# Half-width tiles and half-width statistics at three norms of a two-block transformer kernel on one NeuronCore

## What is computed

```python
def _rmsnorm(x, g):
    xf = x.astype(jnp.float32)
    y = xf * lax.rsqrt(jnp.mean(xf * xf, axis=-1, keepdims=True) + NORM_EPS)
    return (y * g.astype(jnp.float32)).astype(x.dtype)

        x = x + g1 * y
        h = _rmsnorm(x, norm2_g[i]) * (1.0 + sc2) + sh2
        x = x + g2 * _swiglu(h, ffn_w_gate[i], ffn_w_up[i], ffn_w_down[i])
```

## Time and profile before

| | |
|---|---|
| median of three executions | 1727.47 us |
| the profiled execution | 1725.33 us |
| its span, first to last instruction | 1723.5 us |
| mean granted TensorE clock | 0.994 |
| TensorE matmuls busy | 1685.5 us, 98% |
| VectorE busy | 1015.4 us, 59% |
| ScalarE busy | 702.4 us, 41% |
| GpSimd busy | 77.3 us, 4% |
| TensorE's share of the chain that ended last | 89% |

### The profile page before, as it was taken

One profiled execution on the slowest core, in us unless ns is written; L12 is line 12 of the kernel. 1 busy time (PEld: TensorE's weight loads), 2 busy tenths in 40 slices (PEclk: granted clock), 3 DMA queues, 4 the chain that ended last, 5 costly groups with the idle time before them and its releaser, 6 DMA issues.

```text
span 1723.5 us, 23287 instructions
## 1 busy us (share of the span) xinstructions
PE 1685.5 (98%) x7891; PEld 1342.7 (78%) x7891; DVE 1015.4 (59%) x2004; ACT 702.4 (41%) x1329; POOL 77.3 (4%) x62
## 2 busy tenths in 40 slices
PE   9999999999999998889999999999999999999999
PEld 7677777778887776567888888887888888888887
DVE  7788776665466788835655563467444633333334
ACT  5364776663344335753333323234223433332322
POOL 0020000000000073100000000000000000000000
PEclk9999999999999999999999999999999999999999
DMA  6453344444332121002555553353233233332333
GB/s 242 159 160 113 138 156 147 147 147 153 98 98 62 37 86 38 1 25 74 174 194 193 195 198 121 122 183 87 97 99 98 77 99 96 96 101 93 98 98 110
DMA packets 56776, 202.84 MB, mean 118 GB/s; under 512 B 6576, under 2 KB 6704, under 8 KB 56560
## 3 DMA queue, kind: packets, MB, share of 16 engines
q1 hardware_dynamic: 56688, 201.68, 35.7%
HBM read 198.38 MB, written 2.10 MB: 116 GB/s over the span
## 4 chain that ended last, share of the span: by engine, by line
PE 89%; DVE 6%; ACT 2%; issue 2%; DMA 1%; SPq 0%; POOL 0%; DVEq 0%; ACTq 0%; POOLq 0%
PE bank L481 26%; PE bank L483 25%; PE bank L482 25%; PE bank L608 2%; PE bank L663 2%; PE bank L642 1%; PE bank L524 1%; PE bank L525 1%; DVE W_lo L1466 1%; PE bank L539 1%; DVE SB L2075 1%; DVE AW L1480 1%; PE bank L755 1%; PE bank L774 1%; PE bank L527 1%
## 5 line engine op out<-in xcount | busy, mean ns | idle before, releaser
L481 PE MATMUL bank<-H_hi,W_hi 128*128 128x512 f32 x1336 | 534.0, 400 | 3.4 <-DVE W_lo L1466 2.2
L483 PE MATMUL bank<-H_hi,W_lo 128*128 128x512 f32 x1336 | 521.2, 390 | 0.0
L482 PE MATMUL bank<-H_lo,W_hi 128*128 128x512 f32 x1336 | 521.2, 390 | 0.0
L1466 DVE TENSOR_TENSOR W_lo<-RAW,W_hi 128x512 fp32r<-128x512 f32 x538 | 351.4, 692 | 173.7 <-ACT W_hi L951 157.5
L951 ACT ACTIVATE W_hi<-RAW 128x512 fp32r<-128x512 f32 x538 | 317.2, 625 | 264.7 <-PE bank L483 235.3
L481 PEld LDWEIGHTS bank<-H_hi,W_hi 128*128 128x128 f32 x1336 | 251.3, 188 | 74.0 <-issue 20.0
L482 PEld LDWEIGHTS bank<-H_lo,W_hi 128*128 128x128 f32 x1336 | 251.5, 188 | 54.4 <-issue 4.5
L483 PEld LDWEIGHTS bank<-H_hi,W_lo 128*128 128x128 f32 x1336 | 251.2, 188 | 53.4
L481 PE MATMUL bank<-A_hi,W_hi 128*128 128x512 f32 x352 | 136.9, 389 | 0.0
L483 PE MATMUL bank<-A_hi,W_lo 128*128 128x512 f32 x352 | 136.9, 389 | 0.0
L482 PE MATMUL bank<-A_lo,W_hi 128*128 128x512 f32 x352 | 136.9, 389 | 0.0
(11 more groups left out here) (272 smaller groups left out, 2069.2 us busy)
## 6 DMA issues: line engine op xcount, KB each, us to landing
RAW<-weights SPq DMA_DIRECT2D x269, 512.0 KB, 3.7
AW<-ada SPq DMA_DIRECT2D x100, 512.0 KB, 3.7
X<-x_t SPq DMA_DIRECT2D x4, 512.0 KB, 6.2
y_t<-X SPq DMA_DIRECT2D x8, 256.0 KB, 2.0
LW<-lru_w SPq DMA_DIRECT2D x1, 1024.0 KB, 12.8
QX<-QR SPq DMA_DIRECT2D x40, 16.0 KB
CROW<-crow SPq DMA_DIRECT2D x1, 512.0 KB, 10.9
ROPE<-rope SPq DMA_DIRECT2D x1, 512.0 KB, 13.6
```

Source lines behind the costliest of these rows:

```text
L481: pe.matmul(dst, wh, ch(hi, k), start=(k == 0), stop=False)
L482: pe.matmul(dst, wh, ch(lo, k), start=False, stop=False)
L483: mm = pe.matmul(dst, wl, ch(hi, k), start=False, stop=(k == chunks - 1))
L1466: dve.tensor_tensor(W_lo[:, w], RAW[:, c:c + HALF], W_hi[:, w], ALU.subtract).then_inc(lo_done, 1)
```

## The change

The last two residual tiles (6 and 7) and the pair behind the norm are each done in two halves of 256 tokens. The order on TensorE becomes: tile 6 low, tile 7 low, tile 6 high, tile 7 high, pair low, pair high, with the sums and the transposes of a half (2 fp32 matmuls each) put between chunks. Each half has its own sum, root, inverse and row. The high halves of the residual tiles go to banks 5 and 7, the rows to banks 2 and 6. VectorE and ScalarE make H_hi and H_lo in 16 half chunks, with G1 as a ring of four. An activation with Sqrt on one column is put ahead of the split of tile 7. W_lo of the pair's two tiles is made on GpSimd in place of VectorE, four operations of 512 columns at each norm. `norm_stat` is gone with its `busy` matmuls, at the first norm of the kernel also. Cut to the core:

```diff
-            def norm_stat(z, tile, need=None):
-                if tile is not None:
-                    busy(5, tile)
-                square_sums(z, (ch(SQ, 1),), True, need)
-                busy(4, tile)
-                pe.wait_ge(rinv_done, z + 1)
-                stat_rows((z % 2) * 24 + 16, 2).then_inc(stat_mm, 1)
-                busy(5, tile)
+            def first_norm_stat(need):
+                square_sums(0, (ch(SQ, 1),), True, need)
+                pe.wait_ge(rinv_done, 1)
+                stat_rows(16, 2).then_inc(stat_mm, 1)
+
+            def half_sums(squares, e, half, last):
+
+                if last:
+                    pe.wait_ge(sqr_done, 10 * e + 8 + 2 * half)
+                else:
+                    pe.wait_ge(ssr_step, 8 * e + 7 + half)
+                for n in (2 * half, 2 * half + 1):
+                    mm = pe.matmul(ps[4][:, n:n + 1], squares[:, n * P:(n + 1) * P], cs("sel_all"),
+                                   start=(n == 0 and not last), stop=last, skip_group_check=True)
...
+            def three(dst, tile, k, hi, lo, half, chunks, h=None):
...
+                if k % 4 == 0 and half == 0:
+                    pe.wait_ge(lo_done, tile.n * 2 + k // 4 + 1)
+                if h is not None:
+                    pe.wait_ge(h_hi_done, h)
+                pe.matmul(dst, wh, hi, start=(k == 0), stop=False)
+                pe.matmul(dst, wl, hi, start=False, stop=False)
+                if h is not None:
+                    pe.wait_ge(h_lo_done, h)
+                return pe.matmul(dst, wh, lo, start=False, stop=(k == chunks - 1))
+
+            def residual_halves(t0, e, hi, lo, chunks=KC):
+
+                for half in range(2):
+                    for q in (6, 7):
...
+                        for k in range(chunks):
+                            at = k * S + half * 2 * P
+                            mm = three(dst, tile, k, hi[:, at:at + 2 * P], lo[:, at:at + 2 * P], half, chunks)
...
+                            if q == 7 and half == 0 and k == chunks - 2:
+                                half_sums(SS, e, 0, False)
+                            if q == 6 and half == 1 and k == 2:
+                                half_sums(ch(SQ, 1), e, 0, True)
+                            if q == 7 and half == 1 and k == 0:
+                                half_rows(e, 0)
...
+            def pair_halves(t0, e):
...
+                    for k in range(KC + 2):
+                        if k < KC:
+                            mm = part(ps[PAIR_BANK], a, k)
...
+                        if k >= 2:
+                            mm = part(ps[b.bank], b, k - 2)
+                        if half == 0:
+                            if k == 0:
+                                half_sums(SS, e, 1, False)
+                            if k == 2:
+                                half_sums(ch(SQ, 1), e, 1, True)
+                            if k == 5:
+                                half_rows(e, 1)
...
 (ScalarE)
+                for k in range(6):
                     split_hi(Tile(t0 + k + 1))
...
+                    act.activation(ch(SQ, k % 2), ch(X, k), ACT.Square).then_inc(sqr_done, 1)
+                a, b, third = Tile(t0 + 8), Tile(t0 + 9), Tile(t0 + 10)
+                act.activation(VQ[:, 192:193], cs("sel_all"), ACT.Sqrt)
+                split_hi(Tile(t0 + 7), fn=ACT.Identity)
+                act.wait_ge(ssr_step, 8 * e + 6)
+                square_half(6, 0)
+                square_half(7, 0)
+                root_half(0)
+                split_hi(a, fn=ACT.Identity)
+                square_half(6, 1)
+                hi_half(0)
+                hi_half(1)
+                split_hi(b, (0,), ACT.Identity)
+                hi_half(2)
+                square_half(7, 1)
+                hi_half(3)
+                split_hi(b, (1,), ACT.Identity)
+                root_half(1)
+                for u in range(4, 15):
+                    hi_half(u)
+                split_hi(third, (0,), ACT.Identity)
+                hi_half(15)
...
 (GpSimd)
+            for t0 in (T_FFN0, T_CONV, T_FFN1):
+                for tile in (Tile(t0), Tile(t0 + 1)):
+                    for half in range(2):
+                        sl = (2 * tile.slot + half) % 4
+                        pool.wait_ge(hi_done, tile.n * 2 + (half + 1))
+                        c = tile.slot * TILE + half * HALF
+                        w = slice(sl * HALF, (sl + 1) * HALF)
+                        pool.tensor_tensor(W_lo[:, w], RAW[:, c:c + HALF], W_hi[:, w], ALU.subtract).then_inc(lo_done, 1)
...
 (VectorE, residual, behind the six full tiles)
+                split_lo(Tile(t0 + 7))
+                if e == 1:
+                    modulation(1)
+                x_half(6, 0)
+                sum_half(0)
+                x_half(7, 0)
+                variance_half(0)
+                inverse_half(0)
+                x_half(6, 1)
+                t1_half(0)
+                t1_half(1)
+                lo_half(0)
+                sum_half(1)
+                t1_half(2)
+                lo_half(1)
+                x_half(7, 1)
+                t1_half(3)
+                lo_half(2)
+                t1_half(4)
+                variance_half(1)
+                lo_half(3)
+                inverse_half(1)
+                for u in range(5, 16):
+                    t1_half(u)
+                    lo_half(u - 1)
+                lo_half(15)
+                split_lo(Tile(t0 + 10), (0,))
```

More of the change, by code:

```diff
@@ new lines, in pair_halves, with part @@
+            def pair_halves(t0, e):
+                a, b = Tile(t0), Tile(t0 + 1)
+                pe.wait_ge(bank_free[b.bank], b.uses)
+                for half in range(2):
+                    cols = slice(half * 2 * P, (half + 1) * 2 * P)
+                    def part(dst, tile, k):
+                        at = k * S + half * 2 * P
+                        return three(dst[:, cols], tile, k, H_hi[:, at:at + 2 * P], H_lo[:, at:at + 2 * P], half, KC,
+                                     16 + 16 * e + 8 * half + k + 1)
+                    for k in range(KC + 2):
+                        if k < KC:
+                            mm = part(ps[PAIR_BANK], a, k)
+                            if half == 1 and k % 4 == 3:
+                                mm.then_inc(used, 1)
+                        if k >= 2:
+                            mm = part(ps[b.bank], b, k - 2)
+                        if half == 0:
+                            if k == 0:
[4 more added lines that the diff above has]
+                                half_rows(e, 1)
+                mm.then_inc(used, 2)
@@ L897, in _ @@
             pe.wait_ge(pt_last, 2)
[L898 to L901, removed]
+            for q in range(6):
+                linear(Tile(T_AO2 + q), YA_hi, YA2_lo, first=(lambda k: (y_lo_done, 32)) if q == 0 else None)
+            residual_halves(T_AO2, 0, YA_hi, YA2_lo)
             def segment(t0, bodies, hi, lo, chunks=KC, first=None, pair=None, sums=None):
                 def body(i, f, s=None):
-                    for q in range(4):
-                        linear(Tile(t0 + q, i), hi, lo, chunks, first=f if q == 0 else None,
-                               between=early_sums(s) if q == 3 and s is not None else None)
+                    for q in range(4 if s is None else 2):
+                        linear(Tile(t0 + q, i), hi, lo, chunks, first=f if q == 0 else None)
+                    if s is not None:
+                        residual_halves(t0, s, hi, lo, chunks)
                 if pair is not None:
-                    linear_pair(t0, pair)
+                    pair_halves(t0, pair)
                     linear(Tile(t0 + 2), hi, lo, own=False)
@@ L930, in ffn @@
                                 first=lambda k, need=need: (a_lo_done, need + k + 1),
[L931 to L935, removed]
+                                sums=1 if layer == 0 and g == 2 else None)
+            ffn(T_FFN0, 0, 0, 16)
+            segment(T_CONV, 4, H_hi, H_lo, pair=1)
             segment(T_CONVB, 2, H_hi, H_lo)
-            segment(T_CO, 2, B_hi, B_lo, first=lambda k: (a_lo_done, 16 + 22 + k + 1), sums=5)
-            norm_stat(5, Tile(T_FFN1))
-            ffn(T_FFN1, 1, 4, 16 + 22 + 8)
+            segment(T_CO, 2, B_hi, B_lo, first=lambda k: (a_lo_done, 16 + 22 + k + 1), sums=2)
+            ffn(T_FFN1, 1, 2, 16 + 22 + 8)
         @block.scalar
```

160 lines of the change are left out of this document (118 added, 42 removed).

## The result

The changed kernel takes 1736.69 us (median of 4 runs, 1736.07 to 1738.17) against 1727.35 us (1725.78 to 1728.51) for the kernel before on the same chip: ratio 1.0062, 95% interval 1.0049 to 1.0074. It is slower by 9.3 us; 7 were forecast, inside the range. The profiled execution took 1736.07 us with a span of 1734.3, so its span is 10.8 us longer; the profiled execution before was 2.1 us under its median.

What follows compares the result with a forecast made beforehand. TensorE's matmuls are busy 98% of the span; the pair's end hangs on VectorE's last H_lo. Terms -0.2 + 1.5 + 4.3 + 1.2 = +6.9 us take 1725.33 to 1732.2; median 2.1 above, 1734.4 predicted, range 1726 to 1740.

Steps and rivals of the forecast that it cites:

- First G: At the third norm, VectorE's first G comes 10.8 us behind tile 6's first matmul, 6.3 us earlier than before.
- Prices of halves: In the pair, half a G or H_lo takes 0.485 us, a half chunk 0.79; half_sums 0.5, two transposes 0.25.
- rival C: Halves cost VectorE half (0.375 us) and GpSimd does not hold it up: faster, down to 1721; chance 0.10.
- GpSimd holds VectorE up: At the norms, each W_lo on GpSimd delays a following H_lo: three norms +5.7 us, +1.1 if undisturbed.
- rival A: GpSimd does not hold VectorE up: norms 29.7, 29.0, 28.5, +1.1 us, 1729.8 in all; chance 0.21.
- Table and W_lo: Root's table load ahead of tile 7's split makes TensorE wait for W_lo, 1.4 us at first norm, 2.1 at second.
- The clock: Low TensorE clock inside the pair stood only in rival B, at two of three norms, +2.5 us.
- The walk: Step-by-step timing from tile 6's first matmul to behind the pair: norms 31.1, 30.6 and 29.95 us.
- rival B: TensorE's clock falls inside the pair and TensorE falls back: +2.5 us at two of three norms, 1737; chance 0.17.
- The start: At norm 0, without nine unread matmuls the clock stays at 1.2 GHz longer: +1.2 us, bounds -0.25 and +2.8.
- The sum: Over the kernel, -0.2 (third norm) + 1.5 (first) + 4.3 (second) + 1.2 (start) = +6.9 us.

Runs made afterwards that it cites:

- gp_narrow: Changed kernel with each of GpSimd's W_lo operations for the pair covering 16 columns in place of 512, the rest left out; 1728.80 us, ratio 1.0010.
- table_early: Changed kernel with the Sqrt on one column moved from behind the sixth square to behind the third; 1733.50 us, ratio 1.0038.
- c_ve: Changed kernel with the Sqrt behind the third square, high half's sums and transposes earlier on TensorE, pair's W_lo on VectorE; 1729.46 us, ratio 1.0020.
- pair_fill: Changed kernel with unread 512-column matmuls (1, 3, 4, 3) ahead of TensorE's waits for H_lo 1 to 4 in the pair's low half; 1733.58 us, ratio 1.0043.
- ve_lo: Changed kernel with the pair's W_lo made on VectorE again and GpSimd's loop taken out; 1733.78 us, ratio 1.0049.
- c_pieces: Changed kernel with the Sqrt behind the third square, high sums and transposes earlier, W_lo on GpSimd in 128-column pieces; 1724.61 us, ratio 0.9992.

## Why the prediction was right, and where it was off

- **First G** at 12.23, 11.54 and 10.80 us, walked at 12.0, 11.2 and 10.8. Right.
- **Prices of halves**: H_lo 0.47 to 0.48 unheld, G 0.474, a half chunk 0.79, the sums and transposes as taken. Right; rival C had no ground.
- **GpSimd holds VectorE up**: 0.20, 0.75 and 0.57 at the third norm (1.5 together, 1.5 forecast). The mechanism is shown by gp_narrow, and rival A falls. Its own price is 4.9 us over the three norms, against the 4.6 between A's norms and the forecast's; taking it away gave 8.3, since the clock came back with it.
- **Table and W_lo**: 1.49 and 2.21 against 1.4 and 2.1, shown by table_early. Right.
- **The clock, the step that failed.** The walk put the forecast and rival B side by side as alternatives. In the changed kernel both hold: the H_lo late by GpSimd make TensorE wait, and the clock falls at 3 of 3 norms, where B had 2. Its cost is a wait of VectorE of 1.45 for the high row, where the walk had none (0.26 with the clock up). Most of the +1.2, +1.9 and +0.9 by which the distances exceed 31.1, 30.6 and 29.95 is that; in the second norm 0.4 more of holding up than the walk's 1.5 (the sum of squares alone is held for 1.06) and 0.4 more of waiting for the high sums (1.29) come to it. B had the price of a norm right (1.25, against 1.2 measured) by a way that the changed kernel does not go, TensorE's falling back; c_ve's third norm goes it.
- **The start**: +1.2 forecast, +1.6 in the first pair, +0.83 left at tile 6 of the first norm, none in the timed runs. The term was right for the pair and wrong for the whole. Without it the forecast is +5.7 against a measured +9.3, so it stood in for a part of the clock's cost that the walk left out: that the sum came as near as 6.9 is in part luck.
- **The sum**: norms +5.7 forecast and +9.8 in the profile; the median's +9.3 is less than the profile's +10.8 because the profiled execution before was a fast one.
- Open: why the clock fell at each norm. That waits of TensorE have a part in it is shown from both sides, by gp_narrow (shorter waits, and the clock up at two norms) and by pair_fill (the waits filled, and the clock up in the pair at all three), both at 0.993 in the timed executions against 0.988. That GpSimd's holding up is needed for it is not shown: ve_lo and c_ve have none and low stretches still, and c_ve's first and third norm have the same waits and only one of them a low clock.

## What to carry to other kernels

If a change makes the engine at the bound wait in short pieces, price the waits at the low clock too: here they cost once as waits (4.9 us) and again through the clock (3.4), by way of whatever stands behind TensorE in its order. Before moving an operation with two SBUF inputs to GpSimd, look at which of VectorE's operations run beside it, small ones too, and put statistics that another engine waits for ahead of bulk work in TensorE's order. One profiled execution is not enough to tell two such edits apart: look at the clock of all timed ones.

## What the runs showed of the hardware

- **The spread of this kernel's times goes with TensorE's clock.** Over 86 executions of the kernel before on the chips of these runs, means by granted clock:

```
clock   executions   mean us
0.996        7       1723.7
0.995        9       1724.6
0.994       26       1725.9
0.993       21       1726.7
0.992       21       1728.1
0.991        2       1728.6
```

  A thousandth of clock goes with 1.1 us. The changed kernel's four executions had 0.987 to 0.988, some 0.0055 under these; by that slope (an estimate, since waits lower the clock and cost time by themselves) about 6 of its 9.3 us go with the clock. This slope says what goes together and not what causes what: the traces put 3.4 us of waiting at the norms down to it.
- Low stretches of 3.4 to 6.8 us far from the change come and go between executions and variants (at 159.7 before, at 669.1 and 723.8 after), so a difference of some 1 us at one place need not reach the total.
- Operations of 128 columns on GpSimd hold a following VectorE operation for at most 0.3 us, whole ones of 512 for up to 1.06 (the sum of squares of 0.42 that took 1.48); four pieces take 1.7 to 2.1 us instead of 1.28. A VectorE operation with one input from PSUM beside a whole one is not longer (G, 0.87 for two).
- Which waits bring the clock down and which don't stays open: c_pieces kept 1.00 over a wait of 0.87, and c_ve had none and 6.8 us of low clock at two norms with the same waits of 0.87 and 0.52. One norm at the low clock for 6.8 us costs 1.2 (pair_fill) to 1.6 us (c_ve).
